# Moving the first main projection tile in between the index scores

## Time and profile before

| | |
|---|---|
| median of three runs | 3272.89 us (3272.27 to 3274.21) |
| profiled execution, its own time | 3276.17 us |
| its span, first to last instruction | 3274.6 us |
| mean granted clock of TensorE | 0.986 |
| TensorE busy | 3146.4 us (96%) |
| VectorE busy | 1703.6 us (52%) |
| ScalarE busy | 755.9 us (23%) |
| GpSimd busy | 249.7 us (8%) |
| chain that ended last | TensorE 88%, DMA 4%, SP's queue 3%, VectorE 2% |

### The profile page before, as it was taken

The page is one execution under the profiler, slowest core; times in us unless marked ns, Lnnn a source line. Parts: engine busy times, 40 slices in busy tenths (PEclk is TensorE's granted clock), DMA queues, the critical chain, the costliest instruction groups (busy, mean ns, idle before and its releaser), DMA issues.

```text
span 3274.6 us, 52366 instructions
## 1 busy us (share of the span) xinstructions
PE 3146.4 (96%) x20707; PEld 2980.8 (91%) x20707; DVE 1703.6 (52%) x2401; ACT 755.9 (23%) x1214; POOL 249.7 (8%) x422
## 2 busy tenths in 40 slices
PE   5889999999999999999999999899989899999997
PEld 4769999999999999999999999667766899999997
DVE  4478888511332455545555455456544553654654
ACT  5230000011000111111111110443423333333332
POOL 3100000000000000000000000122113110010000
PEclk8999999999999999999999999999999999999998
DMA  9832222222222213223233234741259685584772
GB/s 314 281 115 80 66 85 66 72 66 72 59 78 59 92 59 114 76 86 116 72 105 97 85 91 133 216 111 55 84 148 304 197 273 136 188 254 122 211 208 76
DMA packets 523277, 419.28 MB, mean 128 GB/s; under 512 B 19868, under 2 KB 492188, under 8 KB 519900
## 3 DMA queue, kind: packets, MB, share of 16 engines
q1 hardware_dynamic: 501604, 339.48, 36.6%
q0 software_dynamic: 21568, 78.45, 6.5%
HBM read 345.28 MB, written 74.68 MB: 128 GB/s over the span
## 4 chain that ended last, share of the span: by engine, by line
PE 88%; DMA 4%; SPq 3%; DVE 2%; issue 1%; ACT 1%; POOL 0%; DVEq 0%; ACTq 0%; POOLq 0%
PE banks L282 18%; PE banks L284 18%; PE banks L283 18%; PE banks L1570 6%; PE banks L1572 6%; PE banks L1571 6%; PE banks L758 4%; PE banks L791 3%; PE banks L780 1%; PE banks L390 1%; DMA u_raw<-in_w_out 1%; SPq L922 1%; DMA pool_k<-in_cache_k 1%; DMA x_in<-in_x_prompt 1%; SPq L920 1%
## 5 line engine op out<-in xcount | busy, mean ns | idle before, releaser
L282 PE MATMUL banks<-h_hi,w_hi 128*128 128x352 f32 (+1 forms) x3552 | 1162.5, 327 | 0.0
L284 PE MATMUL banks<-h_hi,w_lo 128*128 128x352 f32 (+1 forms) x3552 | 1158.3, 326 | 0.0
L283 PE MATMUL banks<-h_lo,w_hi 128*128 128x352 f32 (+1 forms) x3552 | 1157.4, 326 | 0.0
L282 PEld LDWEIGHTS banks<-h_hi,w_hi 128*128 128x128 f32 x3552 | 666.9, 188 | 3.1 <-issue 3.0
L283 PEld LDWEIGHTS banks<-h_lo,w_hi 128*128 128x128 f32 x3552 | 669.2, 188 | 0.0
L284 PEld LDWEIGHTS banks<-h_hi,w_lo 128*128 128x128 f32 x3552 | 666.2, 188 | 0.0
L273 DVE TENSOR_TENSOR w_lo<-w_raw,w_hi 128x2048 fp32r<-128x2048 f32 (+1 forms) x78 | 177.7, 2278 | 645.1 <-ACT w_hi L268 521.7
L361 ACT ACTIVATE col<-banks 128x384 f32<-128x384 f32 x150 | 71.2, 475 | 1024.0 <-PE banks L284 984.4
L1625 DVE MAX8 best<-work 128x8 f32<-128x1088 f32 x224 | 289.3, 1292 | 10.1
L1627 DVE MATCH_REPLACE8 work<-best,work 128x1088 f32<-128x1088 f32 x224 | 285.9, 1276 | 0.0
L268 ACT CAST w_hi<-w_raw 128x2048 fp32r<-128x2048 f32 (+1 forms) x78 | 147.9, 1897 | 570.9 <-PE banks L284 520.5
(11 more groups left out here) (260 smaller groups left out, 3512.7 us busy)
## 6 DMA issues: line engine op xcount, KB each, us to landing
w_raw<-in_w_in SPq DMA_DIRECT2D x77, 1024.0 KB, 5.7
u_raw<-in_w_out SPq DMA_DIRECT2D x96, 512.0 KB, 5.4
scratch_proj<-col POOLq DMA_DIRECT2D x76, 544.0 KB, 3.0
ada_w<-in_w_ada SPq DMA_DIRECT2D x16, 2048.0 KB, 15.0
u_raw<-in_w_pb SPq DMA_DIRECT2D x48, 512.0 KB, 4.6
gate_w<-in_w_ada SPq DMA_DIRECT2D x16, 1024.0 KB, 7.7
u_raw<-in_w_pa SPq DMA_DIRECT2D x48, 256.0 KB, 3.3
gates<-scratch_proj SPq DMA_DIRECT2D x64, 192.0 KB, 2.5
```

The costliest lines, as they stand in the source:

```text
L282: nc.tensor.matmul(dst, w_hi[:, par, k, 0:width], h_hi[:, k, a:b], start=(k == 0), stop=False)
L283: nc.tensor.matmul(dst, w_hi[:, par, k, 0:width], h_lo[:, k, a:b], start=False, stop=False)
L284: mm = nc.tensor.matmul(dst, w_lo[:, par, k, 0:width], h_hi[:, k, a:b], start=False, stop=(k == KT - 1))
```

## The change

- The samples' scores come first: `PICKS = [QT, 2, ..., 7]`. `SLOT` keeps each page's place in `scratch_score`.
- The first main tile (3) is split behind the second head of the samples and is no longer computed in the main loop. `main_pieces` computes it in 48 pieces (a piece is the three products of one k block and one chunk), in banks 5, 6 and 7, a number of them behind each pair of prompt heads (`MAIN_PIECES`), twelve behind the last. VectorE leaves it from these banks (`b0`).
- Prompt heads have banks 0 to 4 left: up to 512 columns `n % 4`, above that `2 * (n % 2)`. So a pair of a wide tile waits for both relus of the pair before (`relu_set >= n`) where a narrow one waits for those of the pair before that.
- The second main tile (4) is loaded into `w_second`, the place of `past_t[1]` and of its own `w_lo`, as soon as the samples' scores are made; ScalarE casts it ahead of tile t = 6, VectorE subtracts ahead of t = 7. Its products come behind the pieces and wait for all relus.
- The first pair of the main loop is written out for ScalarE and VectorE, the first tile pair for TensorE. VectorE leaves tile 3 with its four rounds, then splits tile 5 and leaves tile 4.

```diff
@@ split_hi, split_lo
-            raw = w_first if isinstance(t, int) and t == N_IDX else w_raw
+            raw = {N_IDX: w_first, N_IDX + 1: w_second}.get(t, w_raw) if isinstance(t, int) else w_raw
@@ products
-                need(pe, chunk_free, 3 * t + c - 2)
+                if isinstance(t, int) and t == N_IDX + 1:
+                    pe.wait_ge(relu_set, IH * len(PICKS))
+                else:
+                    need(pe, chunk_free, 3 * t + c - 2)
@@ new function
+        def main_pieces(pe, pieces):
+            for x in pieces:
+                k, c = x // 3, x % 3
+                a, b = CHUNKS[c]
+                dst = banks[:, MAIN_BANK + c, 0:b - a]
+                nc.tensor.matmul(dst, w_hi[:, 1, k, :], h_hi[:, k, a:b], start=(k == 0), stop=False)
+                nc.tensor.matmul(dst, w_hi[:, 1, k, :], h_lo[:, k, a:b], start=False, stop=False)
+                mm = nc.tensor.matmul(dst, w_lo[:, 1, k, :], h_hi[:, k, a:b], start=False, stop=(k == KT - 1))
+                if k == KT - 1:
+                    mm.then_inc(chunk_done, 1)
@@ order and banks
-        PICKS = [*range(2, QT), QT]
+        PICKS = [QT, *range(2, QT)]
+        SLOT = lambda t: t - 2
-        pick_bank = lambda n: 3 * (n % 2) if PICKS[n // IH] == QT else 2 * (n % 4)
+        def pick_bank(n):
+            t = PICKS[n // IH]
+            return 3 * (n % 2) if t == QT else n % 4 if WIDTH_OF(t) <= 512 else 2 * (n % 2)
+        MAIN_BANK = 5
+        MAIN_PIECES = {(2, 2): 2, (3, 0): 3, (3, 2): 3, (4, 0): 3, (4, 2): 3, (5, 0): 4, (5, 2): 4, (6, 0): 4, (6, 2): 5,
+                       (7, 0): 5, (7, 2): 12}
@@ VectorE, index_scores
-                if t == QT:
-                    split_lo(dve, N_IDX, N_IDX % 2)
+                if t == QT - 1:
+                    split_lo(dve, N_IDX + 1, 0)
...
                     n += 1
+                    if n == 2:
+                        split_lo(dve, N_IDX, 1)
@@ SP
             sp.dma_start(w_first[:], w_in[:, 0:P].rearrange("(k p) n -> p k n", p=P)).then_inc(w_landed, 16)
+            sp.wait_ge(score_done, IH)
+            sp.wait_ge(w_hi_set, N_IDX + 1)
+            sp.dma_start(w_second[:], w_in[:, P:2 * P].rearrange("(k p) n -> p k n", p=P)).then_inc(w_landed, 16)
...
             sp.wait_ge(acc_stored[1], 16 * 3)
-            load_tile(sp, N_IDX + 1, w_in[:, P:2 * P])
@@ ScalarE
-                if t == QT:
-                    split_hi(act, N_IDX, N_IDX % 2)
+                if t == QT - 2:
+                    act.wait_ge(score_done, IH)
+                    split_hi(act, N_IDX + 1, 0)
...
+                    if n == 2:
+                        split_hi(act, N_IDX, 1)
...
-                with act.Fori(0, pairs - last) as i:
+                if first == T_QA:
+                    split_hi(act, first + 2, first % 2)
+                with act.Fori(int(first == T_QA), pairs - last) as i:
@@ VectorE, first run
-                with dve.Fori(0, pairs - last) as i:
+                if first == T_QA:
+                    for u in range(2):
+                        t, par = first + u, (first + u) % 2
+                        if u:
+                            split_lo(dve, t + 1, 1 - par)
+                        leave_rotated(dve, t, par, 0, rotated + 3 * u, HD // 2, between=pick_round,
+                                      b0=0 if u else MAIN_BANK)
+                        for c in range(ROUNDS - 3):
+                            pick_round(dve)
+                with dve.Fori(int(first == T_QA), pairs - last) as i:
@@ TensorE: the samples' heads now stand ahead of this loop
-            for t in PICKS[:-1]:
+            for t in PICKS[1:]:
                 width = WIDTH_OF(t)
                 for h0 in range(0, IH, 2):
-                    need(pe, relu_set, n - 2)
+                    pe.wait_ge(relu_set, n - 1 if n == IH else n - 2 if width <= 512 else n)
...
                     n += 2
+                    more = MAIN_PIECES.get((t, h0), 0)
+                    if more and not piece:
+                        pe.wait_ge(relu_set, IH)
+                        pe.wait_ge(w_lo_set, N_IDX + 1)
+                    main_pieces(pe, range(piece, piece + more))
+                    piece += more
-            pe.wait_ge(relu_set, n - 1)
-            with pe.Fori(0, N_MAIN // 2) as i:
+            products(pe, N_IDX + 1, 0)
+            with pe.Fori(1, N_MAIN // 2) as i:
```

More of the change, by code:

```diff
@@ L361, in leave_act, with leave_rotated @@
                 nc.scalar.activation(col[:, par, a:b], banks[:, b0 + c, 0:b - a], func).then_inc(chunk_free, 1)
-        def leave_rotated(dve, t, par, earlier, rotated, half, rows=P, plain=0, between=None):
+        def leave_rotated(dve, t, par, earlier, rotated, half, rows=P, plain=0, between=None, b0=0):
             need(dve, col_stored[par], 16 * earlier)
@@ L2097, in _ @@
             pe.wait_ge(idx_copied, 8)
-            n = 0
-            for t in PICKS[:-1]:
+            for h in range(IH):
+                need(pe, relu_set, h - 1)
+                half = slice(ID * (h % 2), ID * (h % 2) + ID)
+                for a in range(0, PAST, 512):
+                    for j in range(NB // 2):
+                        nc.tensor.matmul(banks[32 * j:32 * j + 32, pick_bank(h) + a // 512, :], qi_own[:, h, j, :],
+                                         past_t[j // 2][:, j % 2, a:a + 512], start=True, stop=True)
+                for j in range(NB // 2):
+                    c0 = SEQ + 16 * j
+                    mm = nc.tensor.matmul(banks[32 * j:32 * j + 16, pick_bank(h) + 2, 0:SMP], qi_t[half, h // 2, c0:c0 + 16],
+                                          ki_two[half, SEQ:TOK], start=True, stop=True)
+                mm.then_inc(score_done, 1)
+            n, piece = IH, 0
+            for t in PICKS[1:]:
                 width = WIDTH_OF(t)
                 for h0 in range(0, IH, 2):
-                    need(pe, relu_set, n - 2)
+                    pe.wait_ge(relu_set, n - 1 if n == IH else n - 2 if width <= 512 else n)
                     for a in range(0, width, 512):
@@ L2112, in _ @@
                     n += 2
-            for h in range(IH):
-                need(pe, relu_set, n - (h > 0))
-                half = slice(ID * (h % 2), ID * (h % 2) + ID)
-                for a in range(0, PAST, 512):
-                    for j in range(NB // 2):
-                        nc.tensor.matmul(banks[32 * j:32 * j + 32, pick_bank(n) + a // 512, :], qi_own[:, h, j, :],
-                                         past_t[j // 2][:, j % 2, a:a + 512], start=True, stop=True)
-                for j in range(NB // 2):
-                    c0 = SEQ + 16 * j
-                    mm = nc.tensor.matmul(banks[32 * j:32 * j + 16, pick_bank(n) + 2, 0:SMP], qi_t[half, h // 2, c0:c0 + 16],
-                                          ki_two[half, SEQ:TOK], start=True, stop=True)
-                mm.then_inc(score_done, 1)
-                n += 1
-            pe.wait_ge(relu_set, n - 1)
-            with pe.Fori(0, N_MAIN // 2) as i:
+                    more = MAIN_PIECES.get((t, h0), 0)
[6 more added lines that the diff above has]
+            with pe.Fori(1, N_MAIN // 2) as i:
                 for u in range(2):
```

9 lines of the change are left out of this document (5 added, 4 removed).

## The result

The changed kernel takes 3279.43 us (median of 12 runs, 3277.88 to 3285.51); the kernel before, on the same chip, 3272.88 us (12 runs). The ratio is 1.0020, 95% interval 1.0012 to 1.0029: +6.55 us, where +5.6 was forecast (3278.5 us). It lies inside the range and right on the 0.2% line. In a second set of runs it was 3281.26 against 3272.83, ratio 1.0026 (1.0014 to 1.0038).

A forecast was written before the change was run, and what follows sets the result against it. TensorE, busy 96% of the span, was taken as the bound; the third tile 3.9 us later plus 1.7 us of low clock made +5.6 us on 3272.89, so 3278.5 us, range 3271 to 3284.

The forecast's parts named there:

- The mechanism: TensorE wins 6.5 us by the first tile, VectorE's accumulation ends 12.7 later, using up 6.6 us slack before the third tile.
- The score stage: Samples' heads and prompt pairs with pieces: cycles (4,0) to (7,0) sum to 24.5 us, change-overs 0.8; acc_set 249.2, tile 250.9.
- The way through HBM: From the accumulation's end, the last page's store and first page's load into work take 13.3 us again, landing at 262.5.
- Rival (c): Store and load through HBM take 9.7 us, not 13.3, giving 3274.9 us; chance 0.12 with smaller errors in that direction.
- VectorE's chain: After the page lands, VectorE owes 22.4 us before the third tile: first tile with rounds 18.4, subtraction 2.3, rotations 1.7.
- The low clock: After TensorE's stop of about 10.4 us ahead of the third tile, the half clock costs 1.7 us, bounds 0 and 5.
- The later tiles, the attention and the merge are all chained to TensorE and move with it: Behind the third tile nothing more is lost, so the sum stays +5.6 us.
- The bounds: acc_set within 1.3 us and restart costing 1 to 2.6 us give 3276.5 to 3279.4 us; chance 0.42.
- (a): Clock falls inside the score stage or stays low longer after the long stop: 3280 to 3282 us; chance 0.28.
- (b): VectorE's end stays hidden, acc_set before 245.3, third tile could start at 274.6: -6.5 us, 3266.4 us; chance 0.10.
- (d): Pieces do not overlap the relus in the scores: up to 1.5 us more in some cycles, 3283 and over; chance 0.08.

The follow-up runs named there:

- e1: Changed kernel with VectorE's four pick rounds of the first main tile deferred, five instead of four with each of tiles 5 to 8; 3269.69 us, ratio 0.9993 to the kernel before.
- e2: Changed kernel with the first score page loaded once the last scores are computed, and the first tile's pick rounds ahead of its rotations; 3269.04 us, ratio 0.9990.
- e3: Changed kernel with 40 idle matmuls of 384 columns between TensorE's second and third main tile, filling its stop; 3275.97 us, ratio 1.0008 to the kernel before.
- e7: e2 with three of the last twelve pieces moved behind pair (2,2), ahead of (3,0); 3271.66 us, ratio 0.9996 to the kernel before.
- e9: The kernel of e2 unaltered, run again; 3271.07 us, ratio 0.9992 to the kernel before.
- e5: Changed kernel with all 48 pieces behind the last pair of scores and none between; 3293.99 us, ratio 1.0068 to the kernel before.
- e8: The kernel of e7 unaltered, run again; 3271.04 us, ratio 0.9988 to the kernel before.
- e10: Kernel before with only the samples' scores first and the first tile split behind their second head, waiting for all 28 relus; 3279.89 us, ratio 1.0021.

## Why the prediction came out right, point by point

- **The mechanism** was as forecast: TensorE wins in the scores, VectorE's end moves 13 us, the chain behind it takes all of its slack, the third tile starts late and at a low clock. e1 and e2 show the place from two sides, e3 the clock.
- **The score stage.** Heads every 2.08 us; cast of w_first at 204.4; stop ahead of (3,0) 1.46 us (1.8 forecast); acc_set 249.8 (249.2); first tile done at 251.7 (250.9). The seven cycles from (4,0) to (7,0) took 26.1 us (217.66 to 243.76), not 24.5, so 0.8 us for the change-overs was too small.
- **The way through HBM** was mis-sized: 11.9 us, not 13.3. The load took 4.4 us in place of 5.5; why is not shown, since w_raw ran beside it in both. Rival (c) had the direction, but not the way: its 3.1 us for the store is the median of seven in the earlier trace rows, and the one that counts, the last, took 6.7 us before and 6.5 now.
- **VectorE's chain** took 21.7 us, not 22.4: the first pair of tiles is written out now, the rotations wait 0.17 us for issue, where in the loop they wait 0.3, and the 0.50 us ahead of the subtraction are gone.
- These two, less the 0.6 us of acc_set, made the third tile 2.5 us late instead of 3.9, and the stop 8.0 instead of 10.4.
- **The low clock** cost 2.1 us (1.7). The fourth tile is 4.8 us late by the distances, against 5.6.
- **"The later tiles, the attention and the merge are all chained to TensorE and move with it"** is the step that did not hold. The changed kernel is 4.5 to 4.8 us late up to the attention, and its two profiled attentions are 1 to 2 us longer, while the medians differ by 6.55. So the sum, +5.6, lies near by two errors of opposite sign, 0.8 us too much in the stage and, as far as two profiles of each kernel show, 1 to 2 us in the attention that the prediction put at nothing; that it came so near is luck. The attentions of e1, e2, e7 and e9 are longer as well, which explains in part why these, 4.8 to 5.2 us ahead up to the attention, are only 1.2 to 3.3 ahead in the medians.
- **The bounds.** With acc_set up to 1.3 us later and the restart up to 2.6 us, the forecast's own upper bound is 3280.7, not 3279.4. The measured 3279.43 lies between the two.
- **Rivals.** (a) did not happen in the score stage, where the clock stayed at 1.00; it did in e5, without pieces, and in e8 and e10, each time behind a stop of 2 us or more. (b) needed acc_set before 245.3 and had no chance at 249.8. (d) is refuted by the window with 29.8 of 29.8 us.

The versions with the early page (e2 and e9, e7 and e8) have ratios of 0.9988 to 0.9996; two of the four intervals end below 1. That is 0.1% or less, under what was called measurable here, and e1 is no worse (0.9993). In the distance from the first score to the attention they beat both kernels, by 3.1 to 5.2 us and 7.9 to 10.0 us.

## What to carry to other kernels

When one engine is the bound and the change lets another finish later, add up everything that the second one owes before the first needs it again, the round through HBM included, and set it against the slack. Here 6.6 us of slack stood against 13. Then ask whether the thing waited for exists already: the first page had been in HBM for over 30 us, and a load placed ahead of the last store gave back more than the change had cost. When a part of a combined change is tried alone, its waits have to fit it: in e10 most of the tile's stop of 3.4 us was for relus of banks that it does not write, and so the run leaves open what the order costs.

## What was not expected of the hardware

- In the scores TensorE's clock stayed at full behind single stops of up to 1.8 us (1.5 in the changed kernel, 1.7 in e7, 1.8 in e5) and was at half behind stops of 2.0 and 2.7 us (e5), 2.1 (e8, e10) and 3.1 (before). How long it stayed low differed: 3.4 us in e8, with dense work behind the stop, 21 us in e5, where stops of 0.7 to 1.6 us followed.
- With a fetch of instructions of 0.02 MB beside a store of 544 KB the store landed after 4.7 and 5.2 us in place of 3.0 (e7, e8).
- The kernel before had 0.99 in the window 2080 to 2095 in both executions, and its attention within 0.3 us; in the changed kernel, which gets there 4.6 us later, the same 15 us ran at 0.54. Yet the same kernel can have either: 0.50 in e7 and 1.00 in e8 for the same 13.7 us of the attention.
